# The residual of the output projection turned by TensorE instead of VectorE

## The reference

```
proj = rmsnorm(x, norm_mix) @ w_in           # then gated DeltaNet heads -> o, short convolution -> y_sc
x = x + concatenate([o, y_sc]) @ w_out       # output projection and residual: this stage is changed
u_ff = relu(rmsnorm(x, norm_mlp) @ w_up)
x = x + (u_ff * u_ff) @ w_down               # MLP, width 4096
x = x + sigmoid(rmsnorm(x, norm_ple) @ w_ple_gate) * (p @ w_ple_proj)
y = rmsnorm(x, norm_f)                       # also returned: the new conv and DeltaNet states
```

## Time and profile before

| | |
|---|---|
| median of three runs | 1523.38 us |
| profiled execution | 1522.49 us, its span 1520.7 us |
| busy: TensorE, weight loads | 97%, 95% of the span |
| busy: VectorE, ScalarE, GpSimd | 48%, 31%, 16% |
| output projection on TensorE | from 532.4 to 628.0 us of the span |
| landing of a w_out panel, of an x_col block (median) | 4.1 us, 2.6 us |

### The profile page before, as it was taken

One profiled execution on the slowest core, in us unless ns is written; L12 is line 12 of the kernel. 1 busy time (PEld: TensorE's weight loads), 2 busy tenths in 40 slices (PEclk: granted clock), 3 DMA queues, 4 the chain that ended last, 5 costly groups with the idle time before them and its releaser, 6 DMA issues.

```text
span 1520.7 us, 24673 instructions
## 1 busy us (share of the span) xinstructions
PE 1479.3 (97%) x9324; PEld 1449.6 (95%) x9324; DVE 734.0 (48%) x1313; ACT 474.0 (31%) x854; POOL 246.6 (16%) x306
## 2 busy tenths in 40 slices
PE   7999899899999999999999999999999999999997
PEld 6999898699999989999999999999999999998997
DVE  5676943287685553543333333333333334335525
ACT  6323343233243332533122130221203122135525
POOL 3200311143535363100000000000000000041303
PEclk9999998799999999999999999999999999999999
DMA  7112211412122344111111111111111111112102
GB/s 176 49 36 57 76 51 47 133 35 71 29 84 83 87 98 86 42 56 42 42 42 56 42 42 56 42 42 42 56 42 42 56 42 42 56 42 64 35 28 114
DMA packets 166315, 89.83 MB, mean 59 GB/s; under 512 B 50763, under 2 KB 160267, under 8 KB 166230
## 3 DMA queue, kind: packets, MB, share of 16 engines
q1 hardware_dynamic: 165222, 84.89, 20.1%
q0 software_dynamic: 1008, 3.79, 0.6%
HBM read 77.97 MB, written 10.69 MB: 58 GB/s over the span
## 4 chain that ended last, share of the span: by engine, by line
PE 88%; DVE 5%; issue 2%; POOL 2%; ACT 1%; DMA 0%; DVEq 0%; POOLq 0%; SPq 0%
PE pg L695 66%; PE pg L813 12%; PE bk L870 1%; DVE act_lo L1973 1%; PE bk L884 1%; PE bk L888 1%; PE bk L1021 1%; PE bk L840 1%; POOL act_lo L2296 1%; DVE cv L1621 0%; PE bk L854 0%; PE bk L933 0%; PE bk L930 0%; PE bk L938 0%; PE bk L921 0%
## 5 line engine op out<-in xcount | busy, mean ns | idle before, releaser
L695 PE MATMUL pg<-act_hi,w_hi 128*128 128x352 f32 x1344 | 436.1, 325 | 8.0 <-issue 3.6
L695 PE MATMUL pg<-act_lo,w_hi 128*128 128x352 f32 x1344 | 432.3, 322 | 0.0
L695 PE MATMUL pg<-act_hi,w_lo 128*128 128x352 f32 x1320 | 423.7, 321 | 0.0
L695 PEld LDWEIGHTS pg<-act_hi,w_hi 128*128 128x128 f32 x1344 | 253.1, 188 | 11.3 <-issue 7.3
L695 PEld LDWEIGHTS pg<-act_lo,w_hi 128*128 128x128 f32 x1344 | 253.7, 189 | 0.0
L695 PE MATMUL pg<-u_hi,w_hi 128*128 128x352 f32 x768 | 249.3, 325 | 0.0
L695 PE MATMUL pg<-u_hi,w_lo 128*128 128x352 f32 x768 | 248.9, 324 | 0.0
L695 PEld LDWEIGHTS pg<-act_hi,w_lo 128*128 128x128 f32 x1320 | 248.0, 188 | 0.0
L695 PE MATMUL pg<-u_lo,w_hi 128*128 128x352 f32 x768 | 247.8, 323 | 0.0
L1150 ACT ACTIVATE w_hi<-w_raw 128x1024 fp32r<-128x1024 f32 x111 | 117.0, 1054 | 350.4 <-PE pg L695 320.1
L2337 POOL TENSOR_TENSOR ssq<-ssq,sq 128x352 f32<-128x352 f32 x72 | 76.2, 1067 | 875.1 <-ACT sq L1150 874.4
(11 more groups left out here) (331 smaller groups left out, 1655.5 us busy)
## 6 DMA issues: line engine op xcount, KB each, us to landing
w_raw<-in_w_up SPq DMA_DIRECT2D x32, 512.0 KB, 4.0
w_raw<-in_w_down SPq DMA_DIRECT2D x32, 512.0 KB, 3.3
w_raw<-in_w_in SPq DMA_DIRECT2D x29, 512.0 KB, 4.4
x_tok<-in_x_prompt SPq DMA_DIRECT2D x8, 512.0 KB, 7.4
w_raw<-in_w_out SPq DMA_DIRECT2D x8, 512.0 KB, 4.1
x_col<-in_x_prompt SPq DMA_DIRECT2D x32, 128.0 KB, 2.6
w_raw<-in_w_ple_gate SPq DMA_DIRECT2D x8, 512.0 KB, 3.9
out<-y_tok SPq DMA_DIRECT2D x8, 512.0 KB, 2.9
```

The costliest lines, as they stand in the source:

```text
L695: last = mm(pg[bank][:, 0:TH], w, a, start=i == 0, stop=i == len(terms) - 1)
```

## The change

TensorE transposes the residual. `load_xcol` now loads 128 features with tokens on the partitions, [128 tokens, 9 tiles, 128 features], by 2 DMAs. After each group n of a panel TensorE transposes the 352 tokens of this third into bk[n] (`turn_residual`): the thirds cut the tiles of 128 tokens, so it takes 3 pieces (128, 128, 96 tokens) after the first group, 4 (32, 128, 128, 64) after the second and 4 (64, 128, 128, 32) after the third. ScalarE copies bk[n] into xres (`residual(n)`), and VectorE's add of third n waits for the copy (xr_copied). VectorE's transposes are gone, and its panels and SP's loads become loops. SP waits for the transposes of panel j - 2 (xcol_turned) before it loads x_col for panel j; before, it waited for VectorE's transpose of that block.

```
-            def load_xcol(x, j):
-                for b in range(4):
-                    f = slice(j * P + 32 * b, j * P + 32 * b + 32)
-                    dst = x_col[x][32 * b:32 * b + 32, :]
-                    sp.dma_start(dst[:, 0:TP].rearrange("i (q j) -> i q j", j=32),
-                                 x_p[0, :, f].rearrange("(q i) j -> i q j", i=32)).then_inc(xcol_in[x], 16)
-                    sp.dma_start(dst[:, TP:T], x_s.rearrange("b t d -> (b t) d")[:, f]).then_inc(xcol_in[x], 16)
+            def load_xcol(x, i):
+                f = ds(i * WIDE + x * P, P)
+                sp.dma_start(x_col[x][:, 0:NTT, :], x_p[0].rearrange("(t p) d -> p t d", p=P)[:, :, f]) \
+                    .then_inc(xcol_in[x], 16)
+                sp.dma_start(x_col[x][0:TS, NTT, :], x_s.rearrange("b t d -> (b t) d")[:, f]) \
+                    .then_inc(xcol_in[x], 16)
...
-            for i in range(1, KD // 2):
+            with sp.Fori(1, KD // 2) as i:
                 for x in range(2):
-                    load_w(U_OUT + x, i, wout_v[:, :, i * WIDE + x * P:i * WIDE + (x + 1) * P], KD)
-                    sp.wait_ge(sm.x_blocked, 2 * i + x - 1)
-                    load_xcol(x, 2 * i + x)
+                    load_w(U_OUT + x, i, wout_v[:, :, ds(i * WIDE + x * P, P)], KD)
+                    sp.wait_ge(sm.xcol_turned, at(x - 1, i, 2))
+                    load_xcol(x, i)
...
+            pieces = [[(0, 0, 128, 0), (1, 0, 128, 128), (2, 0, 96, 256)],
+                      [(2, 96, 128, 0), (3, 0, 128, 32), (4, 0, 128, 160), (5, 0, 64, 288)],
+                      [(5, 64, 128, 0), (6, 0, 128, 64), (7, 0, 128, 192), (8, 0, 32, 320)]]
+
+            def turn_residual(x, i, n):
+
+                pe.wait_ge(sm.consts_made, 3)
+                pe.wait_ge(xcol_in[x], at(32, i, 32))
+                for t, a, e, c in pieces[n]:
+                    last = turn(bk[n][:, c:c + e - a], x_col[x][a:e, t, :], ident[a:e, a:e])
+                last.then_inc(sm.xcol_turned if n == 2 else sm.xcol_turned3, 1)
+
             def out_unit(x, i):
                 b = U_OUT + x
                 panel_ready(b, i)
                 for n in range(3):
                     group(b, i, 4 * n, 4, n, parts(b % 2, KD, 0, act_hi, act_lo, n))
+                    turn_residual(x, i, n)
...
@@ ScalarE, out_pair(i)
                 for x in range(2):
                     b = U_OUT + x
+                    def residual(n):
+
+                        act.wait_ge(sm.xcol_turned if n == 2 else sm.xcol_turned3,
+                                    at(x + 1, i, 2) if n == 2 else at(2 * x + n + 1, i, 4))
+                        act.wait_ge(sm.consts_made, 3)
+                        op(xres[:, ds(2 * i + x, 1), cols(n)].rearrange("p a t -> p (a t)"), bk[n][:, 0:TH],
+                           ACT.Copy).then_inc(sm.xr_copied, 1)
+
                     splits = last and x == 1
+                    residual(0)
+                    residual(1)
+                    if not splits:
+                        residual(2)
                     act.wait_ge(sm.sample_states_out, 16 * H)
...
                         if splits:
                             split_x(n_mlp, n)
+                            if n == 0:
+                                residual(2)
...
@@ VectorE, out_pair(i)
                     for n in range(3):
                         product_ready(b, i, 4 * n + 4)
-                        if n == 0:
-                            dve.wait_ge(sm.x_blocked, at(x + 1, i, 2))
+                        dve.wait_ge(sm.xr_copied, at(3 * x + n + 1, i, 6))
                         x_t = rows(xres[:, ds(2 * i + x, 1), cols(n)])
                         tt(x_t, x_t, pg[n][:, 0:TH], ADD).then_inc(sm.evacuated, 4)
...
-                    if x == 0:
-                        x_blocks(1, i)
-                    elif i < KD // 2 - 1:
-                        x_blocks(0, i + 1)
```

More of the change, by code:

```diff
@@ L180, in __init__ @@
         self.mix_hi = sem("mix_hi")
-        self.x_blocked = sem("x_blocked")
+        self.xcol_turned = sem("xcol_turned")
+        self.xcol_turned3 = sem("xcol_turned3")
+        self.xr_copied = sem("xr_copied")
         self.x_made = sem("x_made")
@@ L367, in trunk @@
         qkv_room = sb("qkv_room", [P, NQ, T], scope=late)
-        x_col = [sb(f"x_col{i}", [P, T], scope=late) for i in range(2)]
+        x_col = [sb(f"x_col{i}", [P, NTT + 1, P], scope=late) for i in range(2)]
         late.close()
@@ L643, in _ @@
                     for x in range(2):
-                        load_xcol(x, x)
+                        load_xcol(x, 0)
                 for b, n in thirds(a, e):
@@ L1052, in _ @@
                 last.then_inc(sm.mm_done, 4)
+                turn_residual(0, 0, n)
             out_unit(1, 0)
@@ L1977, in rows @@
                 return ap.rearrange("p a t -> p (a t)")
[L1979 to L1987, removed]
             def out_pair(i):
@@ L1993, in out_pair @@
                         product_ready(b, i, 4 * n + 4)
-                        if n == 0:
-                            dve.wait_ge(sm.x_blocked, at(x + 1, i, 2))
+                        dve.wait_ge(sm.xr_copied, at(3 * x + n + 1, i, 6))
                         x_t = rows(xres[:, ds(2 * i + x, 1), cols(n)])
                         tt(x_t, x_t, pg[n][:, 0:TH], ADD).then_inc(sm.evacuated, 4)
-                        if i == KD // 2 - 1 and x == 1:
+                        if isinstance(i, int) and x == 1:
                             split_x(n_mlp, n, 0)
                     unit_done(b, i)
-                    if x == 0:
-                        x_blocks(1, i)
-                    elif i < KD // 2 - 1:
-                        x_blocks(0, i + 1)
-            for i in range(KD // 2):
+            with dve.Fori(0, KD // 2 - 1) as i:
                 out_pair(i)
+            out_pair(KD // 2 - 1)
             ups = 0
```

## The result

The changed kernel takes 1544.5 us (median of four, 1543.4 to 1545.0) against 1524.1 us for the kernel before in the same session: a ratio of 1.0134, 95% interval 1.0116 to 1.0151. The forecast said 1538.6 us with a range up to 1542.5. The direction was right and the mechanisms were the ones named; the size was 6 us short.

The account below looks back on a forecast made before the run. The prediction took TensorE to bound the projection stage; 0.8 us (first panel), 9.8 (panels 2 to 7) and 4.6 (last panel) summed to 15.2 us more, giving 1538.6 us, range 1533.5 to 1542.5.

Parts of the forecast that it names:

- TensorE is the bound and pays in full: Output projection stage: only TensorE sets the time, busy 80.35 of 80.35 us; work put on it is paid in full.
- VectorE's transposes were worth nothing: Output projection stage: VectorE's eight transposes of 1.27 us each lie under matmuls; taking them away returns nothing.
- First panel, 0.8: First projection panel: third group's transposes and the copy-and-add path end together, costing 0.8 us (0.7 to 1.1).
- Price of a full transpose, 0.108: TensorE in each panel: four full transposes cost 0.43 us, 0.108 each; six in a panel 0.65 us.
- Price of a short one: TensorE in each panel: 0.062 us a body plus 0.16 for height change, four short pieces, 0.64 a panel for changes.
- upper bound of 12.6: Panels 2 to 7: highest added time for the six together, against 9.8 us forecast and 6.0 at the low end.
- 12.5 to 13.2: Sign of a right forecast: us from one panel's first matmul to the next's, instead of 11.44.
- Last panel, 4.6: Last panel into the MLP: ScalarE's first square waits for two copies and starts 4.6 us later (4.2 to 4.8).
- One: Rival, TensorE's short pieces: they pay no change of height; 10.9 us more, 1534.3 us; chance 0.17.
- Two: Rival, ScalarE's copies come too late in every panel, 2 us in each of seven; 1552 us; chance 0.04.
- three: Rival, TensorE's granted clock falls to 0.50; one panel there costs 9.5 us more, 1548 us; chance 0.04.
- four: Rival, not slower: transposes slip under weight loads and the end chain has slack; 1523.4 us; chance 0.03.

Follow-up runs that it names:

- e_one_piece: Changed kernel with TensorE turning only the first full tile of each third; copies, additions, waits and transfers stay: 1531.1 us, 1.0047 of before.
- e_best: Changed kernel with e_full's and e_order's edits together, and in the first panel a third's transposes ahead of its products: 1532.1 us, 1.0052 of before.
- e_full: Changed kernel with all 11 pieces a panel as whole tiles of 128 tokens, one more transfer filling the last tile: 1536.9 us, 1.0079 of before.
- e_twice: Changed kernel with each of a panel's four short pieces turned twice in a row: 1546.1 us, 1.0146 of before.
- e_adjacent: Changed kernel with the two short pieces of a third side by side, three changes of height instead of four: 1540.9 us, 1.0110 of before.
- e_sixtyfour: e_full with one short piece of 64 tokens in each of two thirds, last in the second, first in the last: 1539.5 us, 1.0104 of before.
- e_single: e_full with one short piece of 32 tokens in each of two thirds, first in the second, last in the last: 1541.3 us, 1.0116 of before.
- e_order: Changed kernel; in the last panel ScalarE does first square and splits before copying the second third, second ones before the last copy: 1541.4 us, 1.0114 of before.

## Why the prediction was right, and where it failed

- **TensorE is the bound and pays in full.** Right. Its stretch stays at 100% busy, and e_one_piece shows that nothing but the pieces adds time.
- **VectorE's transposes were worth nothing.** Right in this: VectorE is busy 7 us less, and e_one_piece, without those transposes too, is no faster than its three pieces a panel allow (0.12 us each over before).
- **First panel, 0.8.** Measured 0.9. That the two paths end together is shown by e_best.
- **Price of a full transpose, 0.108.** Measured 0.11 to 0.12 (e_full 1.26 / 11, e_one_piece 0.36 / 3). Right, to less than 0.1 us a panel.
- **Price of a short one: this step failed.** It took 0.062 for the body and 0.16 for a lone piece's change of height: 0.09 in, 0.07 out. The body is right (0.065 in e_twice) and the way in is right (0.09). The way out costs 0.2, so a lone short piece costs 0.30 on top of its body. Four in a panel are 1.2 us instead of 0.64; six panels of 2.24 us are 13.5 instead of 9.8, and even over the upper bound of 12.6. The panel itself, 13.69, lies above the 12.5 to 13.2 that were to show the forecast right. The sum with the measured terms is 0.9 + 13.5 + 4.6 = 19.0 instead of 15.2. That puts the time at 1542.4, a hair inside the range; what took it out is the 1.4 us outside the stage (below) and a kernel before that was 0.7 slower in the same session (1524.1 against 1523.4).
- **How the step failed.** The earlier trace rows did hold the answer. From 256.26 to 257.78 are 1.52 us, less two steps 1.20 for eight 32-row matmuls. I read 0.02 of a way out in the spacing behind them and wrote down that the rest could not be told apart. But the eight at the 0.062 of the earlier trace rows are 0.50, so 0.70 was unexplained, and that was the upper bound for one way in and out, not 0.22. The measured 0.30 lies inside it. The bound had been set by what was visible and not by what was left over.
- **A closer row was there.** Where the earlier trace rows lies, 24 short transposes stand in the stream in one row, of 32, 24 and 16 rows (L753, L764, L766). The rows at its two ends, in the kernel before:

```profile
28.88 0.32 PE L695 MATMUL pg<-act_lo,w_hi 128*128 128x352 f32 x1
29.14 0.68 PE L753 MATMUL bk<-ident,x_tok 32*128 32x32 f32 x8
...
30.73 0.43 PE L695 MATMUL pg<-act_hi,w_hi 128*128 128x352 f32 x1
30.99 0.32 PE L695 MATMUL pg<-act_lo,w_hi 128*128 128x352 f32 x1
```

  From 28.88 to 30.99 are 2.11 us; two steps of 0.159 and 24 bodies of 0.062 taken off leave 0.30 for one way in and out, which is what a lone short piece then cost. With it the sum would have been about 19 us.
- **The rule.** Four changes of height less in each of two thirds (e_full) give 0.98 us a panel although the pieces are larger; one less in each (e_adjacent) gives 0.41. The Trainium skill (TensorEngine Tiling (Array Packing), Tiling Modes) says: "Changing tiling mode (not just tile) drains the TensorE". The traces agree that the change costs and a second piece of the same height does not; that it is a drain they do not show. Going from 32 rows straight to 64 has a price of its own. In e_sixtyfour the set 64, 128, 128, 128 took 0.69 us; with 32 rows in front and one full piece less it should take 0.64 if that step were free, and in e_adjacent it took 0.74. The other way round, 64 to 32, it is 0.60 (from e_single's 0.65) against 0.75. So a step between the two costs 0.10 to 0.15 us.
- **Height or width.** A short piece also has fewer columns (32x32), and no experiment parts the two. The kernel before does for the way in: a full-height matmul of only 32 columns comes 0.17 us after the last one of its stream, not 0.25. For the way out no run tells.

```profile
105.54 0.33 PE L695 MATMUL pg<-act_hi,w_lo 128*128 128x352 f32 x1
105.71 0.30 PE L792 MATMUL bk<-log_a,m_inc 128*128 128x32 f32 x2
```

- **Last panel, 4.6.** Right to 0.1, and for the reason given: e_order takes 3.2 of it back by moving the copies of the second and the last third one place back in ScalarE's queue. TensorE's waits in it were 1.11 and 1.74 us, where the prediction had about 1.3 and 2.1, since its own transposes took more of the time.
- **Rivals.** One (no change of height) would have had panels of 12.4 (11.44 and 1.0 for the pieces); they are 13.69. Two fell by e_one_piece, three by the granted clock of 1.00, four by the time.
- **Not in the forecast:** about 1.4 us of the 20.4 lie outside the stage. In part they are spread from one execution to the next, and in part they are not explained.

## What to carry to other kernels

Work that is moved to the engine that sets the time costs its own duration and what it does to the stream around it: in a stream of full-height matmuls such as this one, cut transposes at the height of the stream, even where that means transposing rows twice, and where short ones can't be avoided put them next to each other. Put a copy that waits for a later product behind the work that is already ready in an in-order queue. When a trace does not say how a number parts, take the whole unexplained rest as the upper bound.

## What the runs showed of the hardware that I had not expected

- Leaving a piece of 32 or 64 rows costs about 0.2 us, going in 0.09 (e_single, e_sixtyfour); a second piece of the same height behind the first costs 0.065 (e_twice).
- A piece of 96 rows costs no change: the third with 128, 128 and 96 rows took 0.34 us, three full ones in e_full the same 0.34.
- Eleven full transposes with 1408 columns (12.71 us a panel) are faster than eleven partly short ones with 1056 (13.69).
- The trace's idle time of weight loads shows only a part of this: 6.2 us at 32 places, where the changes of height in eight panels cost some 8 x 1.2 = 9.6.
